# Two hand-overs in a peer layer: the order of the expert outputs, and where the first expert row stands

## The reference, cut to what matters

```python
q = (xt @ wq).reshape(T, 8, 2, 128)
s = jnp.einsum('thpc,hpnc->thpn', q, subkeys)          # scores against 128 sub-keys per half
# top 16 per half, 256 sums, top 16 of these: 16 experts per head, gates = softmax(best)
act = jax.nn.gelu(jnp.einsum('cd,ced->ce', xb, ub), approximate=False) * gb
y   = jnp.einsum('ce,ced->cd', act, vb)                # sum over the picked experts
```

## Time and profile before

| | before |
|---|---|
| median of 3 runs | 1741.61 us (1737.21 to 1745.03) |
| profiled execution | 1738.3 us, span 1737.0 |
| TensorE (PE) busy | 96% of the span |
| VectorE, ScalarE, GpSimd busy | 60%, 49%, 37% |
| chain that ended last, by engine | PE 87%, DVE 5%, POOL 3%, ACT 2%, DMA 2% |

### The profile page before, as it was taken

How to read it: one execution, slowest core, us unless ns; L and a number is a source line. 1 busy time by engine, 2 the same in 40 slices (tenths; PEclk the granted TensorE clock), 3 DMA queues, 4 the chain that set the end, 5 groups by cost and what they waited for, 6 DMA issues and landing times.

```text
span 1737.0 us, 29518 instructions
## 1 busy us (share of the span) xinstructions
PE 1669.8 (96%) x11486; PEld 1524.0 (88%) x11486; DVE 1045.6 (60%) x1767; ACT 850.0 (49%) x1253; POOL 637.8 (37%) x799
## 2 busy tenths in 40 slices
PE   7989999999999998997999989999999999999997
PEld 6778999899899988886889989999999888888886
DVE  4565555466555546654144678899878555555555
ACT  5566444343544435564444444454455455555553
POOL 0667100060500016565642454657654322222221
PEclk9999999999999999999999999999999999999999
DMA  8334554555554555342344567666555677777774
GB/s 318 131 129 150 205 186 179 198 202 183 175 214 176 191 191 183 119 149 98 121 149 155 189 200 218 200 197 205 183 184 183 212 243 242 241 241 243 241 243 173
DMA packets 98073, 331.70 MB, mean 191 GB/s; under 512 B 10972, under 2 KB 44284, under 8 KB 79376
## 3 DMA queue, kind: packets, MB, share of 16 engines
q1 hardware_dynamic: 95904, 322.94, 55.0%
q0 software_dynamic: 2032, 6.89, 1.1%
HBM read 310.91 MB, written 18.87 MB: 190 GB/s over the span
## 4 chain that ended last, share of the span: by engine, by line
PE 87%; DVE 5%; POOL 3%; ACT 2%; DMA 2%; issue 1%; SPq 0%; DVEq 0%; ACTq 0%; POOLq 0%
PE banks L985 20%; PE banks L481 12%; PE banks L429 9%; PE banks L431 9%; PE banks L430 9%; PE banks L950 6%; PE banks L952 6%; PE banks L951 6%; PE banks L453 3%; POOL uL L2313 3%; PE banks L939 2%; PE banks L418 1%; DMA raw<-in_qkv 1%; DVE xL L1573 1%; DVE wL L1544 1%
## 5 line engine op out<-in xcount | busy, mean ns | idle before, releaser
L2276 POOL TENSOR_TENSOR wL<-raw,wH 128x256 fp32r<-128x256 f32 x392 | 296.3, 794 | 544.2 <-ACT wH L1010 544.0
L2067 DVE TENSOR_TENSOR uL<-raw,uH 128x1024 fp32r<-128x1024 f32 x192 | 240.8, 1254 | 228.7 <-ACT uH L1471 228.6
L1471 ACT ACTIVATE uH<-raw 128x1024 fp32r<-128x1024 f32 x256 | 270.1, 1056 | 166.7 <-PE banks L985 166.6
L429 PE MATMUL banks<-xH,wH 128*128 128x256 f32 x1216 | 343.3, 282 | 8.0 <-DVE xL L1573 8.0
L430 PE MATMUL banks<-xL,wH 128*128 128x256 f32 x1216 | 342.2, 281 | 0.0
L431 PE MATMUL banks<-xH,wL 128*128 128x256 f32 x1216 | 342.2, 281 | 0.0
L2313 POOL TENSOR_TENSOR uL<-raw,uH 128x256 fp32r<-128x256 f32 x256 | 234.4, 946 | 238.1 <-ACT uH L1471 238.1
L1010 ACT ACTIVATE wH<-raw 128x2048 fp32r<-128x2048 f32 (+1 forms) x154 | 269.9, 1762 | 80.4 <-PE banks L481 68.6
L950 PE MATMUL banks<-xH,uH 128*128 128x256 f32 x1024 | 296.7, 290 | 9.6 <-POOL uL L2313 9.1
L1544 DVE TENSOR_TENSOR wL<-raw,wH 128x2048 fp32r<-128x2048 f32 (+1 forms) x93 | 211.5, 2276 | 134.0 <-ACT wH L1010 133.8
L951 PE MATMUL banks<-xL,uH 128*128 128x256 f32 x1024 | 289.8, 283 | 0.0
(11 more groups left out here) (318 smaller groups left out, 2665.0 us busy)
## 6 DMA issues: line engine op xcount, KB each, us to landing
raw<-in_eu SPq DMA_DIRECT2D x128, 512.0 KB, 4.2
raw<-in_ev SPq DMA_DIRECT2D x128, 512.0 KB, 3.4
raw<-in_gu SPq DMA_DIRECT2D x44, 1024.0 KB, 4.8
raw<-in_dn SPq DMA_DIRECT2D x22, 1024.0 KB, 4.7
gelu_scratch<-st SPq DMA_DIRECT2D x128, 128.0 KB, 4.0
st<-gelu_scratch SPq DMA_DIRECT2D x128, 128.0 KB, 3.3
raw<-in_win SPq DMA_DIRECT2D x14, 1024.0 KB, 4.8
raw<-in_qkv SPq DMA_DIRECT2D x12, 1024.0 KB, 7.4
```

The lines of the kernel that those rows point to most:

```text
L429: e.matmul(o, wh[:, w0:w0 + P], H[:, k, :], start=k == 0, stop=False)
L1471: e.activation(uH[n % US][:, :], raw[k // 2][:, (k % 2) * UW:(k % 2) * UW + UW], ACT.Copy).then_inc(s_uh, 1)
L2067: e.tensor_tensor(uL[n % US][:, :], raw[k // 2][:, (k % 2) * UW:(k % 2) * UW + UW], uH[n % US][:, :].bitcast(F32), ALU.subtract).then_inc( ...
L2276: r = e.tensor_tensor(wL[n % NS][:, d], raw[n % NR][:, d], wH[n % NS][:, d].bitcast(F32), ALU.subtract)
```

## The change

Two edits. In the first, the out loop takes its rows in the order 124, 125, 126, 127, 0, 1, ..., 123 (`out_row`). The GELU results of rows 124 to 127 stay in the four buffers `st`: they are neither written to DRAM nor read back, and the first four gates wait for the GELU itself. `expert_act(0)` and `expert_act(1)` stand in rows 126 and 127 of the expert-in loop instead of 127 and behind it. In the second, ScalarE splits expert rows 0 and 1 inside the query loop (at chunks 6 and 7), each `uL` has a wait for the weight buffer that it overwrites, and TensorE and ScalarE do row 0 ahead of the first group of scores.

```diff
+    def out_row(i):
+        return (P - 4 + i) % P
 # TensorE
         def expert_in(i):
+            if i == 0:
+                e.wait_ge(s_qL, 5)
...
         for i in range(P):
-            if i < 8:
+            if 0 < i < 8:
                 sub_scores(i // 4, i % 4)
             if p["gates"] is not None:
                 gates(p["gates"])
             expert_in(i)
+            if i == 0:
+                sub_scores(0, 0)
 # ScalarE
         def usplit(n):
...
-            if n < US:
-                e.wait_ge(low(NCH - 1), LO[NCH - 1] + 1)
-                e.wait_ge(s_used, NCH - 1)
+            if n < US - 1:
+                e.wait_ge(low(NCH - 1), LO[NCH - 1] + 1)
+            elif n == US - 1:
+                e.wait_ge(s_used, NCH - 2)
...
                 split(pq + c + NS)
+            if c >= 6:
+                usplit(c - 6)
             e.wait_ge(s_used, pq + c + 1)
...
-        for n in range(US - 1):
-            usplit(n)
         for i in range(P):
             usplit(i + US - 1)
-            if i < 8:
+            if 0 < i < 8:
                 sub_scores(i // 4, i % 4)
...
-            if i == P - 1:
-                expert_act(0)
+            if i >= P - 2:
+                expert_act(i - P + 2)
             expert_in(i)
+            if i == 0:
+                sub_scores(0, 0)
...
-        expert_act(1)
 # VectorE: the same move of expert_act, and
             e.wait_ge(s_uh, n + 1)
+            if n == 1:
+                e.wait_ge(s_used, NCH - 1)
 # GpSimd
         def expert_gate(i):
-            e.wait_ge(s_rb[i % 4], 16 * (i // 4 + 1))
+            if i < 4:
+                e.wait_ge(s_ge, out_row(i) + 1)
+            else:
+                e.wait_ge(s_rb[i % 4], 16 * (i // 4))
...
+            e.tensor_tensor(halves(ga[i % NA][:, :]), halves(st[i % 4][:, :]), G[:, :, out_row(i), :], ALU.mult).then_inc(s_ga, 1)
+        e.wait_ge(s_used, NCH - 2)
         usplit(0)
 # SyncE
-            src = a["eu"][n] if n < P else a["ev"][n - P]
+            src = a["eu"][n] if n < P else a["ev"][out_row(n - P)]
...
         def gelu_back(i):
-            e.wait_ge(s_st[i % 4], 16 * (P // 4))
-            if i >= 4:
-                e.wait_ge(s_ga, i - 3)
-            e.dma_start(st[i % 4][:, :], gel[i]).then_inc(s_rb[i % 4], 16)
+            e.wait_ge(s_st[i % 4], 16 * (P // 4 - 1))
+            e.wait_ge(s_ga, i - 3)
+            e.dma_start(st[i % 4][:, :], gel[out_row(i)]).then_inc(s_rb[i % 4], 16)
...
             expert(UR + US - 1 + i)
-            if i == P - 1:
-                gelu_back(4)
-            e.wait_ge(s_ge, i + 1)
-            e.dma_start(gel[i], st[i % 4][:, :]).then_inc(s_st[i % 4], 16)
-            if i >= P - 3:
-                gelu_back(i - P + 3)
-        for i in (3, 5, 6):
-            gelu_back(i)
+            if i < P - 4:
+                e.wait_ge(s_ge, i + 1)
+                e.dma_start(gel[i], st[i % 4][:, :]).then_inc(s_st[i % 4], 16)
+            if i >= P - 2:
+                gelu_back(i - P + 6)
+        gelu_back(6)
```

More of the change, by code:

```diff
@@ L1445, in scalar, with usplit @@
         whole(fill)
+        def usplit(n):
+            if n >= 2 * P:
+                return
+            k = n % UR
+            e.wait_ge(s_u[k], 16 * (n // UR + 1))
+            if n < US - 1:
[3 more added lines that the diff above has]
+            else:
+                sig, v = expert_used(n - US)
+                e.wait_ge(sig, v)
+            e.activation(uH[n % US][:, :], raw[k // 2][:, (k % 2) * UW:(k % 2) * UW + UW], ACT.Copy).then_inc(s_uh, 1)
         pq = first("pq")
@@ L2321, in expert_gate @@
                 e.wait_ge(s_gL, i - NA + 1)
-            e.tensor_tensor(halves(ga[i % NA][:, :]), halves(st[i % 4][:, :]), G[:, :, i, :], ALU.mult).then_inc(s_ga, 1)
+            e.tensor_tensor(halves(ga[i % NA][:, :]), halves(st[i % 4][:, :]), G[:, :, out_row(i), :], ALU.mult).then_inc(s_ga, 1)
+        e.wait_ge(s_used, NCH - 2)
         usplit(0)
```

## The result

The changed kernel takes 1728.32 us in the median of 13 runs (1726.26 to 1736.51), the kernel before 1740.33 in 13 runs beside it (1736.30 to 1754.51). The ratio is 0.9934, with a 95% interval of 0.9919 to 0.9950: 11.5 us faster, 8.7 to 14.1. Forecast were 11.2 us and 1730.4. The profiled execution took 1733.42 with a span of 1732.1, only 4.9 us under the profiled one of before (span 1737.0). So the median moved as forecast and the profile did not, and both need explaining.

What follows compares the result with a forecast made beforehand. TensorE was taken to bound the kernel, with gains only where it stands still or runs at the lower clock. -6.6 and -4.6 us, zero between, gave -11.2: from 1741.6 to 1730.4 us, range 1724 to 1738.

Steps and rivals of the forecast that it cites:

- A: Hand-over from projections to first expert row: 6.6 us go, 2.3 of low clock and 4.3 of TensorE standing still.
- Rival (b): First hand-over keeps its wait because uL 0 is late; -6.6 is lost, 1737 is left; chance 0.06.
- B: Hand-over from last expert-in to first expert-out row: 4.6 us go, 2.91 of idle time and 1.73 of low clock.
- rival (c): Last expert-in to first out row: late gates or uH 130 move TensorE's wait to out row 1 or 2; 1733; chance 0.08.
- Between: Stretch between the two hand-overs: zero change, the middle stall of 4.50 us before 1029.54 stays.
- VectorE's lost lead: Between the hand-overs: VectorE loses some 7.6 us of lead, but that lead is idle time, costing nothing.
- PE waits appear in the middle: Sign that the forecast is wrong: TensorE waits appearing between the two hand-overs; no size given.
- Rival (d): Out rows lose their cadence, GpSimd's gates and VectorE's uL slowing each other; slower, median of 1743; chance 0.04.
- The sum: Whole kernel: -6.6 - 4.6 = -11.2 us, median from 1741.6 to 1730.4.

Runs made afterwards that it cites:

- e_fill: Kernel before, with useless matmuls added in TensorE's waits at both hand-overs; ratio 0.9990 to the kernel before.
- e_late_act: Changed kernel with gH and gL of the first two out rows back where they stood before; ratio 0.9936 to the kernel before.
- e_scores_first: Changed kernel with the first group of scores ahead of expert row 0 again, early splits kept; ratio 0.9960 to the kernel before.
- e_a_only: Kernel before with only the edit at the start of the expert layer, output order and GELU round trip as before; ratio 0.9953.
- e_yield_all: Changed kernel with VectorE waiting for GpSimd's uL ahead of its 128x2048 two-input instructions, both token halves; 1726.28 us, ratio 0.9924 to the kernel before.
- e_after_again: Changed kernel, unchanged, run again for a second profile and more times; ratio 0.9930 to the kernel before.

## Why the prediction was right

- *A, -6.6.* 12.13 - 5.48 = 6.65 measured. Both parts were there: `e_fill` gives 2.2 for the clock (forecast 2.3), and what is left, 4.4, is standing still (forecast 4.3). uL 0 had 2.3 us of slack, row 1's uL 2.8. Rival (b) didn't occur.
- *B, -4.6.* 4.67 measured. `e_fill` gives 1.7 for the clock at B, as forecast (1.73); the DRAM trip of the earlier trace rows is gone. Out rows 1 and 2 found their inputs, so rival (c) didn't occur.
- *Between, zero.* 428.70 before, 428.69 and 428.74 in two profiles after. That VectorE's lost lead was idle time, as forecast, agrees with this, and the 4.51 us wait stayed in its place of the loop. What the prediction did not know is that this stretch has a second outcome, 6.7 to 8.5 us longer, which the profile of before happened not to show and that of after did. It is on the forecast's own list of what would make it wrong ("PE waits appear in the middle") without being an effect of the change: `e_fill` has it without either edit.
- *The first profile.* Its 4.9 us are 0.2 ahead of A, 6.65 at A and 4.7 at B, less 6.7 in the middle.
- *Rival (d).* The out rows kept 2.72 us, and a gate took 0.74 us in the mean (0.76 before).
- *The sum.* -11.2 against 11.5 (8.7 to 14.1). By the lengths it is 6.65 + 4.67 = 11.3. The median, 1728.32, lies 2.1 under the forecast 1730.4; 1.3 of it is that the kernel before came to 1740.33 in 13 runs and not to the 1741.61 of the three that the forecast started from. That so small a sum came out to some tenths, while single executions differ by 5 us and more, is in part luck.

That the spread of the changed kernel's times (eight of 13 at 1726.3 to 1728.5, five at 1731.5 to 1736.5) is this second outcome is likely but only argued: the profiled execution with it took 1733.42, those without it 1728.02 and 1727.20. `e_late_act` shows that another 3 to 5 us can come from elsewhere in the program.

## What to carry to other kernels

At a hand-over between two loops, sum what the next matmul waits for, and add the rows behind the wait that run at the lower clock: here they were about a third of the gain (2.2 + 1.7 of 11.3 us). When a loop ends with its results on chip and the next one reads them back, start the next one with the rows that are still there. And compare two profiles stage by stage before you believe their difference: here an unrelated stall left 4.9 us to be seen of a gain of 11.

## What the runs showed of the hardware

- Not every wait was followed by the lower clock. Behind 1.46 us of idle time matmuls took 0.27, at a granted clock of 1.00 (`e_scores_first`, 935 to 940). In the kernel before, 2.50 us more of idle time followed, with scores between, and matmuls took 0.41, at a granted clock of 0.50 (939.30 to 944.10). Behind 2.00 us (`e_a_only`) the first pairs of matmuls took 0.63 to 0.75, and only those from 1373.29 on, 1.6 us later, 1.05.
- A GpSimd instruction with SBUF inputs can be kept out by VectorE's two-input instructions for their whole run (9.15 us for 0.74 of work), not only for the one that runs. Where a wait cut VectorE's run short, it ended at 5.28 us (`e_yield_all`). The Trainium skill, SBUF — State Buffer, section "Who interferes with whom", calls the ports that the two engines share an exclusive lock, and has a VectorE instruction with two SBUF inputs contend with a GpSimd one that reads SBUF. That the one that issues first holds them for the whole instruction it says of VectorE's 2-port mode. If GpSimd came in at the end of that instruction, the wait would have ended with the `eq` of 2.28 us; in the trace it did not. In `e_after_again` (offset 0.43 us) and `e_a_only` (0.40) the two took turns. What decides between the outcomes was not found.
